# A third input unit in the prologue of a hybrid GLA and pooling block, its own weight place and banks, and another form of the input layer norm

## The reference

```python
xp = layer_norm(x_prompt, ln_in_g, ln_in_b)
xs = layer_norm(x_sample, ln_in_g, ln_in_b)
mod_ctx = jax.nn.silu(c_ctx) @ w_ada[l] + b_ada[l]       # 2048 x 12288
mod_lat = (jax.nn.silu(c) @ w_ada[l] + b_ada[l])[:, None, :]

def block(x, mod, ...):
    sh1, sc1, g1, sh2, sc2, g2 = jnp.split(mod, 6, axis=-1)
    h = x * (1 + sc1) + sh1
    m, s_f, s_b = mixer(h, ...)                          # z = h @ w_in, GLA heads, pooling, @ w_out
    x = layer_norm(ALPHA * x + g1 * m, ln1_g, ln1_b)
    h = x * (1 + sc2) + sh2
    gate, up = jnp.split(h @ w_gu, 2, axis=-1)
    f = (jax.nn.silu(gate) * up) @ w_down
    return layer_norm(ALPHA * x + g2 * f, ln2_g, ln2_b), s_f, s_b

def layer_norm(x, g, b):
    mu = jnp.mean(x, -1, keepdims=True); var = jnp.mean(jnp.square(x - mu), -1, keepdims=True)
    return (x - mu) * lax.rsqrt(var + LN_EPS) * g + b
```

## Time and profile before

| | before |
|---|---|
| median of 3 runs | 2828.46 us |
| profiled execution | 2833.38 us |
| its span | 2831.6 us |
| TensorE busy | 2714.7 us (96%) |
| VectorE busy | 1447.6 us (51%) |
| ScalarE busy | 912.9 us (32%) |
| GpSimd busy | 659.9 us (23%) |
| granted TensorE clock, mean | 0.98 |

### The profile page before, as it was taken

How to read it: one execution, slowest core, us unless ns; L and a number is a source line. 1 busy time by engine, 2 the same in 40 slices (tenths; PEclk the granted TensorE clock), 3 DMA queues, 4 the chain that set the end, 5 groups by cost and what they waited for, 6 DMA issues and landing times.

```text
span 2831.6 us, 37813 instructions
## 1 busy us (share of the span) xinstructions
PE 2714.7 (96%) x16304; PEld 2421.9 (86%) x16304; DVE 1447.6 (51%) x1582; ACT 912.9 (32%) x952; POOL 659.9 (23%) x220
## 2 busy tenths in 40 slices
PE   5798999999998999999999999999999999999997
PEld 2577788879886887999999999999999888888876
DVE  5222232224566547565555565665566545544578
ACT  5232232323222116333333333333333333223343
POOL 0000000000000000344443444444344333333440
PEclk8899999999999997999999999999999999999998
DMA  8864555542247323233333222333322845464576
GB/s 329 297 243 158 184 204 182 202 153 76 97 133 245 127 75 126 82 99 104 104 104 104 89 93 95 104 104 104 104 93 86 292 169 204 171 215 179 178 243 240
DMA packets 179385, 438.13 MB, mean 155 GB/s; under 512 B 9980, under 2 KB 25732, under 8 KB 173076
## 3 DMA queue, kind: packets, MB, share of 16 engines
q1 hardware_dynamic: 176916, 430.48, 44.2%
q10 hardware_dynamic: 2304, 5.24, 0.5%
HBM read 401.83 MB, written 33.85 MB: 154 GB/s over the span
## 4 chain that ended last, share of the span: by engine, by line
PE 56%; DMA 12%; POOL 12%; DVE 11%; issue 4%; ACT 4%; SPq 0%; POOLq 0%; ACTq 0%; DVEq 0%
DMA raw_w<-w_gu_b 7%; PE ps L2175 6%; PE ps L2176 6%; PE ps L2177 6%; PE ps L1845 5%; PE ps L1847 5%; PE ps L1846 5%; PE ps L1898 4%; PE ps L2096 4%; PE ps L2097 4%; PE ps L2098 4%; POOL raw_w L849 4%; DVE w_lo L1503 3%; POOL raw_w L852 3%; POOL low L846 3%
## 5 line engine op out<-in xcount | busy, mean ns | idle before, releaser
L1503 DVE TENSOR_TENSOR w_lo<-raw_w,w_hi 128x1024 fp32r<-128x1024 f32 x264 | 359.3, 1362 | 307.8 <-ACT w_hi L1101 305.3
L1101 ACT ACTIVATE w_hi<-raw_w 128x1024 fp32r<-128x1024 f32 x264 | 269.8, 1054 | 631.6 <-POOL raw_w L855 382.3
L2096 PE MATMUL ps<-x_hi,w_hi 128*128 128x320 f32 x1408 | 437.4, 311 | 3.5 <-DVE w_lo L1503 3.3
L2097 PE MATMUL ps<-x_lo,w_hi 128*128 128x320 f32 x1408 | 436.0, 310 | 0.0
L2098 PE MATMUL ps<-x_hi,w_lo 128*128 128x320 f32 x1408 | 436.0, 310 | 0.0
L846 POOL TENSOR_TENSOR low<-raw_w 128x1024 f32<-128x1024 f32 x42 | 104.1, 2478 | 1091.3 <-DMA raw_w<-w_gu_b 1091.3
L1634 DVE TENSOR_TENSOR x_lo<-low,x_hi 128x2560 fp32r<-128x2560 f32 (+2 forms) x55 | 221.1, 4023 | 260.9 <-ACT x_hi L1186 260.9
L1845 PE MATMUL ps<-x_hi,w_hi 128*128 128x320 f32 x1056 | 343.5, 325 | 6.8 <-DVE x_lo L1306 5.0
L2175 PE MATMUL ps<-w_hi,x_hi 128*128 128x512 f32 x880 | 343.1, 390 | 6.4 <-DVE x_lo L1634 2.4
L2176 PE MATMUL ps<-w_lo,x_hi 128*128 128x512 f32 x880 | 342.4, 389 | 0.0
L2177 PE MATMUL ps<-w_hi,x_lo 128*128 128x512 f32 x880 | 342.4, 389 | 0.0
(11 more groups left out here) (203 smaller groups left out, 4379.1 us busy)
## 6 DMA issues: line engine op xcount, KB each, us to landing
raw_w<-w_gu_b SPq DMA_DIRECT2D x180, 512.0 KB, 5.6
low<-w_ada SPq DMA_DIRECT2D x60, 1024.0 KB, 5.3
raw_w<-w_down SPq DMA_DIRECT2D x55, 1024.0 KB, 5.1
low<-hidden_scratch SPq DMA_DIRECT2D x33, 1280.0 KB, 6.1
raw_w<-w_in_b SPq DMA_DIRECT2D x33, 1024.0 KB, 7.4
high<-w_ada SPq DMA_DIRECT2D x22, 1024.0 KB, 5.4
raw_w<-w_out SPq DMA_DIRECT2D x16, 1024.0 KB, 5.1
x_raw<-w_ada SPq DMA_DIRECT2D x14, 1024.0 KB, 9.4
```

Source lines behind the costliest of these rows:

```text
L1101: nc.scalar.activation(weight(0, w), src, ACT.Copy).then_inc(prod_hi, 1)
L1503: nc.vector.tensor_tensor(weight(1, n), src, weight(0, n).bitcast(F32), ALU.subtract).then_inc(prod_split, 1)
L2096: mm(out, wh, version(v, 0, k), start=first and k == 0, stop=False)
L2097: mm(out, wh, version(v, 1, k), start=False, stop=False)
```

## The change

The third unit (unit 2) joins units 0 and 1 in the prologue (`EARLY = 3`).

- Its parts lie in a place of their own, `low_r` from column 12288 (`W_THIRD`), where the token tiles 1 and 2 were; so its split waits for all turns (`turned` 20). It accumulates in banks 4 and 5 from the start of the second block on, behind `turned_out` 20. Units from 3 on use slot (u - 1) % 2 of `w_hi` and `w_lo`, and all later stages are shifted by one slot likewise.
- Modulation sums use bank 6 alone, and `first_cols` uses bank 7, two column groups in turn. `first_cols(i)` waits for `mod_cols` i, and a new group for the copy of the one before.
- The 32 slices go through six places listed in `FIRST_SLOT`: four at first, slot 4 (one token tile) in place of slot 3 from slice 8, slot 5 (`raw_w[:, 0]`, after unit 2 is split) in place of slot 2 from slice 19, and three places (0, 5, 4) from slice 24 on.
- The order of loads: token tiles 0 and 1, then slices, with the other token tiles after slices 0, 4 and 6, and units 0 to 3 after slices 1, 3, 9 and 27; then unit 4. Tiles are turned after slices 1, 3, 5, 6 and 8.
- The quarters of units 0, 1 and 2 follow slices 3, 5 and 7 of each block from the second.
- Slots 1 and 2 of the second ring overlap unit 2's place, so their first loads wait for `unit_used` 3.
- The input norm: ScalarE takes a square root, VectorE the reciprocal and minus mean times it, ScalarE the Identity.
- ScalarE's order: roots and normalisations of the five tiles, with `first_row(0)` and the split of unit 0 after tile 1, that of unit 1 after tile 3, then `first_row(1)` and the split of unit 2. VectorE: rests of units 0 and 1 after the copies of tiles 2 and 3, that of unit 2 after those of tile 4, ahead of the first `add_bias`.

```diff
@@ -160,8 +160,12 @@
...
 ADA = [(2, "row", 0), (4, "col", SC), (3, "col", SH), (5, "row", 1)]
-X_AFTER = {0: 1, 1: 2, 3: 3, 5: 4}
-TURN_AFTER = {0: 0, 1: 1, 3: 2, 4: 3, 6: 4}
+X_AFTER = {0: 2, 4: 3, 6: 4}
+UNIT_AFTER = {1: 0, 3: 1, 9: 2, 27: 3}
+TURN_AFTER = {1: 0, 3: 1, 5: 2, 6: 3, 8: 4}
+FIRST_SLOT = (0, 1, 2, 3, 0, 1, 2, 3, 4, 0, 1, 2, 4, 0, 1, 2, 4, 0, 1, 5, 4, 0, 1, 5, 4, 0, 5, 4, 0, 5, 4, 0)
+EARLY = 3
+W_THIRD = 12288
 N_ADA = 16
@@ -328,7 +332,15 @@
...
-        return 2 * n + half if n < 2 else (2 * (n - 2) + half) % 3
+        if n < 2:
+            return 2 * n + half
+        return 4 + half if n < EARLY else (2 * (n - EARLY) + half) % 3
...
+    def w_part(part, u):
...
+        if u == 2:
+            return low_r[:, W_THIRD + UNIT * part:W_THIRD + UNIT * part + UNIT]
+        return (w_hi, w_lo)[part][:, u if u < 2 else (u - 1) % 2, :]
@@ -355,18 +367,15 @@
...
             return first_ring[:, at:at + STEP].rearrange("p (k c) -> p k c", k=4)
-        return lo(S_X + (i - 4) * STEP, STEP).rearrange("p (k c) -> p k c", k=4)
...
-    def first_slot_of(i):
...
-        return i % 4 if i < 8 else (4, 5, 6, 0)[i % 4]
+        src = lo(S_X, STEP) if i == 4 else raw_w[:, 0, :]
+        return src.rearrange("p (k c) -> p k c", k=4)
...
-    FIRST_USES = [[i for i in range(FIRST_STEPS) if first_slot_of(i) == n] for n in range(7)]
+    FIRST_USES = [[i for i in range(FIRST_STEPS) if FIRST_SLOT[i] == n] for n in range(6)]
@@ -585,12 +596,14 @@
...
-            n = first_slot_of(i)
+            n = FIRST_SLOT[i]
             before = [j for j in FIRST_USES[n] if j < i]
...
                 sp.wait_ge(first_used, before[-1] + 1)
-            elif n >= 4:
-                sp.wait_ge(turned, (16, 20, 12)[n - 4])
+            elif n == 4:
+                sp.wait_ge(turned, 16)
+            elif n == 5:
+                sp.wait_ge(split_done, 3)
             group, part = SECTIONS[i // 4 % 2][0], i // 8
@@ -605,22 +618,27 @@
...
                 sp.wait_ge(ada_used, i - RING + 1)
+            elif i:
+                sp.wait_ge(unit_used, EARLY)
             sp.dma_start(ring_slot(i), w_ada_v[ADA[a // 4][0], a % 4, i % 4]).then_inc(ada_in[i % RING], 16)
         load_x(0)
-        load_unit(0, w_in_b[0])
+        load_x(1)
         for i in range(FIRST_STEPS):
...
                 load_x(X_AFTER[i])
-            if i == 0:
-                load_unit(1, w_in_b[1])
-        load_unit(2, w_in_b[2])
+            if i in UNIT_AFTER:
+                load_unit(UNIT_AFTER[i], w_in_b[UNIT_AFTER[i]])
+        sp.wait_ge(first_used, FIRST_USES[5][-1] + 1)
+        load_unit(4, w_in_b[4])
         sp.wait_ge(h_split, KT)
...
             g = scan_index(a, b)
+            if kind == "main" and b == 2 and a < 2:
+                continue
             if kind == "main" and b == 2 and a + 3 < N_IN:
@@ -874,27 +892,28 @@
...
             act.wait_ge(raw_in[s], 16 * (u // 2 + 1))
-            if u >= 2:
-                act.wait_ge(unit_used, u - 1)
-            nc.scalar.activation(w_hi[:, s, :], raw_w[:, s, :], ACT.Copy).then_inc(w_hi_done, 1)
+            if u == 2:
+                act.wait_ge(turned, 4 * TT)
+            elif u >= 3:
+                act.wait_ge(unit_used, u - 2 if u < 5 else u - 1)
+            nc.scalar.activation(w_part(0, u), raw_w[:, s, :], ACT.Copy).then_inc(w_hi_done, 1)
...
-        def deviation(t):
-            link(nc.scalar.activation(mv(t, 2), mv(t, 1), ACT.Ln, bias=cols(C_EPS, 1)))
-            link(nc.scalar.activation(mv(t, 2), mv(t, 2), ACT.Exp, scale=-0.5))
-            link(nc.scalar.activation(mv(t, 3), mv(t, 0), ACT.Copy, scale=mv(t, 2)))
-            link(nc.scalar.activation(mv(t, 3), mv(t, 3), ACT.Copy, scale=-1.0))
...
-        def normalise(t, tile, moments_done, n):
...
-            act.wait_ge(moments_done, n)
-            deviation(t)
-            nc.scalar.activation(tile, tile, ACT.Identity, bias=mv(t, 3),
-                                 scale=mv(t, 2)).then_inc(normed, 1)
+        def in_rooted(t):
...
+            act.wait_ge(moments, t + 1)
+            nc.scalar.activation(mv(TT + t, 2), mv(TT + t, 1), ACT.Sqrt, bias=cols(C_EPS, 1)).then_inc(in_root, 1)
...
+        def in_normalise(t):
...
+            act.wait_ge(in_scale, t + 1)
+            tile = lo(S_X + (t % 3) * D, D)
+            nc.scalar.activation(tile, tile, ACT.Identity, bias=mv(TT + t, 3),
+                                 scale=mv(TT + t, 2)).then_inc(normed, 1)
@@ -902,17 +921,21 @@
...
                 act.wait_ge(mod_turned, i - 1)
-            nc.scalar.activation(high[:, at:at + 512], ps[:, 6 + i % 2, :], ACT.Copy).then_inc(mod_rows, 1)
...
-        normalise(TT, lo(S_X, D), moments, 1)
-        split_in(0)
-        normalise(TT + 1, lo(S_X + D, D), moments, 2)
-        split_in(1)
-        for t in range(2, TT):
-            normalise(TT + t, lo(S_X + (t % 3) * D, D), moments, t + 1)
+            nc.scalar.activation(high[:, at:at + 512], ps[:, 6, :], ACT.Copy).then_inc(mod_rows, 1)
...
+        for t in range(TT):
+            in_rooted(t)
+            in_normalise(t)
+            if t == 1:
+                first_row(0)
+            if t in (1, 3):
+                split_in(t // 2)
+        first_row(1)
+        split_in(2)
         for q in range(4):
-            first_row(2 * q)
-            first_row(2 * q + 1)
+            if q:
+                first_row(2 * q)
+                first_row(2 * q + 1)
             for k in range(4 * q, 4 * q + 4):
@@ -998,7 +1021,8 @@
...
                 evac(a)
-                split_in(a + 2)
+                if a != 2:
+                    split_in(a + 3 if a < 2 else a + 2)
             elif kind == "vT":
@@ -1277,6 +1300,10 @@
...
             nc.vector.bn_aggr(mv(TT + t, 0, 2), cols(C_STAT + 24 * (t % 2), 24)).then_inc(moments, 1)
+            dve.wait_ge(in_root, t + 1)
+            link(nc.vector.reciprocal(mv(TT + t, 2), mv(TT + t, 2)))
+            nc.vector.scalar_tensor_tensor(mv(TT + t, 3), mv(TT + t, 0), -1.0, mv(TT + t, 2), ALU.mult,
+                                           ALU.mult).then_inc(in_scale, 1)
@@ -1307,21 +1334,20 @@
...
         ln_in(0)
-        split_rest(0)
-        ln_in(1)
-        evac_turned(0)
-        split_rest(1)
-        for t in range(2, TT):
+        for t in range(1, TT):
             ln_in(t)
             evac_turned(t - 1)
+            if t >= 3:
+                split_rest(t - 3)
         evac_turned(TT - 1)
+        split_rest(2)
         for q in range(4):
...
                 add_bias(section, q, mod_col[:, section, 4 * q:4 * q + 4, :],
-                         ps[:, 4 + g, 0:8].rearrange("p (k c) -> p k c", c=2), mod_cols)
+                         ps[:, 7, 8 * g:8 * g + 8].rearrange("p (k c) -> p k c", c=2), mod_cols)
             dve.wait_ge(mod_cols, 2 * q + 2)
@@ -1832,16 +1858,16 @@
...
                     first, last = b == 0 and k % 4 == 0, b == 3 and k % 4 == 3
-                    wh = w_hi[:, n % 2, k * P:(k + 1) * P]
-                    wl = w_lo[:, n % 2, k * P:(k + 1) * P]
+                    wh = w_part(0, n)[:, k * P:(k + 1) * P]
+                    wl = w_part(1, n)[:, k * P:(k + 1) * P]
                     out = ps[:, main_bank(n, half), 0:HALF]
...
                     xl = x_lo[:, k, half * HALF:(half + 1) * HALF]
-                    if n < 2 and half == 0:
+                    if n < EARLY and half == 0:
                         pe.wait_ge(h_split, k + 1)
-                    if n >= 2 and first:
-                        i = 2 * (n - 2) + half
-                        pe.wait_ge(zin_evac, 1 if i < 2 else 2 if i == 2 else 3 + (i - 3) // 2)
+                    if n >= EARLY and first:
+                        i = 2 * (n - EARLY) + half
+                        pe.wait_ge(zin_evac, 1 if i < 2 else 2 if i == 2 else 4 + (i - 3) // 2)
                     mm(out, wh, xh, start=first, stop=False)
@@ -1854,45 +1880,37 @@
...
             pe.wait_ge(sums_ready, 1)
-            if i < 2:
-                pe.wait_ge(turned_out, 4 * TT)
-            else:
-                pe.wait_ge(mod_cols, i - 1)
+            if i:
+                pe.wait_ge(mod_cols, i)
             for k in range(4):
                 c = PRO_ROW + 512 * (i % 2) + k * P
-                ins = mm(ps[:, 4 + i % 2, 2 * k:2 * k + 2], high[:, c:c + P], group_sum,
+                at = 8 * (i % 2) + 2 * k
+                ins = mm(ps[:, 7, at:at + 2], high[:, c:c + P], group_sum,
                          start=True, stop=True)
...
-        used = [0] * 7
+        used = [0] * 6
         for i in range(FIRST_STEPS):
-            n = first_slot_of(i)
+            n = FIRST_SLOT[i]
             used[n] += 1
-            q, g, m = i // 8, i // 4 % 2, i % 4
+            q, m = i // 8, i % 4
             pe.wait_ge(first_in[n], 16 * used[n])
-            if m == 0 and q:
-                pe.wait_ge(mod_rows, 2 * (q - 1) + g + 1)
-            ada_step(6 + g, first_slot(n), m, first_used)
+            if m == 0 and i:
```

(50 more changed lines are left out.)

## The result

The changed kernel takes 2843.13 us, the median of six runs (2839.70 to 2845.13), against 2828.16 us before (six runs); the ratio is 1.0051 with a 95% interval of 1.0040 to 1.0062. So it is 15 us slower. The direction was as forecast; the size was not: 2835.8 was said, with 2842 as the upper end.

What follows compares the result with a forecast made beforehand. TensorE, 96% busy, was taken to bound the kernel by its matmul order. The prologue to the end of `first_cols(7)` cost +10.4 us, the tail -3.1: +7.3, so 2835.8 us on the median 2828.46; range 2824 to 2842.

Steps and rivals of the forecast that it cites:

- The knot: Before the first block: `first_cols(1)` waits for VectorE's first bias, queued behind the split of unit 2; ends at 66.4 us.
- e1: End of `first_cols(1)` in the prologue, forecast at 66.4 us (65.8 to 67.5).
- e7: End of `first_cols(7)`, forecast at 138.0 us against 127.6 before: +10.4 us.
- The pace of a block: Prologue blocks between `first_cols` ends: TensorE's order, with h tiles awaited, takes 23.5 us, over the 21.7 of loads.
- rival C: Clock falls in every prologue block, 5.1 us instead of 1.5: +10.9, 2839.4 us; chance 0.16.
- Rival A: Loads go on setting the prologue's pace, TensorE's waits overlapping them better: -2.6, 2825.9 us; chance 0.18.
- The tail: From the end of `first_cols(7)` to unit 3's first matmul: 32.7 us against 35.8, so -3.1 us, ring wait included.
- T3: End of unit 2's last quarter, where ring loads may be issued; forecast 19.3 us after `first_cols(7)` ends.
- priced at nothing: Side effects taken as 0, among them one more exp table load before the first gate (0 to 1.3 us).
- the last step of the sum: Whole kernel: +7.3 us laid on the traced execution makes 2840.7 us, on the median 2828.46 makes 2835.8.
- main(3,0): First quarter of unit 3, after the ring's four steps; forecast to start near 170 us, everything later following one to one.
- B: Loads set the pace and TensorE keeps 2.4 GHz through the last quarters: -6.8, 2821.7 us; chance 0.14.

Runs made afterwards that it cites:

- the kernel with the knot cut: Changed kernel with the split of unit 2 (ScalarE and VectorE) moved behind the first four h tiles: 2839.25 us, ratio 1.0039.
- the second trace: The changed kernel run once more, unaltered, for a second trace and more times: median 2842.62 us, ratio 1.0056.
- the quarters left out: Changed kernel without computing the first three quarters of unit 2: 2836.41 us, ratio 1.0034.
- free ring kernel: Changed kernel with first loads of second-ring steps 1 to 3 put in places unit 2 does not use: 2831.62 us, ratio 1.0015.
- three edits: Changed kernel with second ring from quarter 12, unit 2's split behind four h tiles, rests of units 0 and 1 behind tile 3's copies: 2816.50 us, ratio 0.9965.

## Why the forecast had the sign and missed the size

**The knot held, but came later than said.** e1 was to be 66.4 (65.8 to 67.5) and was 68.97; in four other traces of the same prologue it was 67.6 to 68.3. The mechanism is that of the forecast, row by row, and the kernel with the knot cut confirms it. The term mis-sized is the queue before it: turned 16 came at 52.1, not 49.9, since tile 2 was turned from 39.83 on, after a slice at half clock (1.88 us), and VectorE's copies ended at 43.9 instead of 42.1; F8 landed at 57.18 instead of 55.0. That is 2.2 of the 2.6 us, and 2.4 of them reached e7 (140.45 instead of 138.0). The forecast's own addition before e1, 60.6 + 1.9 + 2.3 + 0.2, makes 65.0 and not 65.2; nothing hangs on it.

**The pace of a block held.** Said were 23.5 us and e7 - e1 = 71.6 with 1.5 for the clock. Measured: 24.15, 24.15 and 23.2 us, together 71.5. The clock was at full from 72.7 to 144.4 us, so rival C is refuted for this execution. The half clock of the first 3.7 us of the first block cost nothing that shows, as the second block, at full clock, took as long. So that the total came out right is luck in part: the 1.5 us put down for the clock were spent on two blocks 0.6 us longer each than worked out. In the second trace C happened in part. Rival A (loads set the pace) is refuted by the 309 GB/s and by the quarters left out, which would have gained nothing.

**The tail held.** T3 - e7 was 18.1 instead of 19.3, unit 3 started 12.7 after T3 instead of 12.4, and the half clock behind it took 1.6 instead of 1.0: together 32.4, where 32.7 were forecast. T3 came sooner because the clock was at half for 6.8 us in the last quarters and not for 10.2; in the second trace it was 10.2 again, and T3 - e7 19.1. The free ring kernel shows the wait directly: 11 us, as much as the 11 us of quarters that were moved out of this stretch. Free ring (11 us) and cut knot (3.9) are together the 15 us by which the kernel is slower, if they add; what is left of the change then neither wins nor loses anything that the medians show.

**One thing priced at nothing was not.** The exp table that the old norm left loaded must now be loaded before the first gate: that wait of TensorE for ScalarE was 0.88 us and is 1.7 (waits from 170 us on), and the shift grows there by 0.8 us, from 9.4 to 10.1. The new norm alone in the kernel before shows the same wait of 1.7 us.

```profile
PE ps L2034 <- ACT low L1033: 1.7, 1, 1.7
```

**What failed is the last step of the sum, and two terms before it.** The medians lie 15.0 us apart, where 7.3 were said: 7.7 are missing.

The last step made a difference between traces, +7.3, and laid it on the median by taking the same 4.9 us off both kernels. But an execution's distance from its median is not the same in both. The first trace of before stands 5.2 us above the median of its six runs, that of the changed kernel 2.0 above its own (it is the longest of its six), and the second ones 7.7 and 0.6. That is 3.2 of the missing 7.7 us. In the forecast's own terms, 2840.7 was said for a traced execution and 2845.13 and 2843.19 were measured, 4.4 and 2.5 more.

The 4.4 us of the first trace are terms of the sum. The queue before the knot, in the norm stage, was 2.4 us too short. The tail was 0.4 too long. And "everything later follows main(3,0) one to one, to within 1 us" was 2.4 us too low: 0.8 for the table, and 1.8 that came in small steps between 600 us and the end, less 0.2 between. These 1.8 us are not shown to be of the change: in the second trace the shift shrinks there, from 13.2 to 10.2 us.

So one trace was no base to 0.2%, and the range should have had some 5 us more on its upper side. What sets the length of an execution from 600 us on stays open.

**The rival of the other side** (B, faster by 6.8) needed e7 by 130 us; the earliest with all three units computed was 134.4, after three edits.

## What to carry to other kernels

Moving work under loads pays only if nothing that was issued beside it is now issued behind it: here 11 us of quarters were moved, and the ring that shared their storage made TensorE wait 11 us at a place where it had nothing else to do. When a shorter chain (the norm) or a split is put into an engine's queue, look at what stands behind it there, in order; two such places were mended by moving a few lines, for 6 to 7.6 us together. And before laying a difference from one trace on a median, look where that trace stands among the runs.

## What the runs showed of the hardware

The granted clock made the largest difference between the two traced executions of the changed kernel in the prologue: in the same blocks it stayed at 1.00 for 71.7 us in one and fell to 0.51 twice for 3.4 us in the other, both times while a quarter's matmuls came one h tile at a time. Where loads depend on TensorE's use of their places, such a stretch can cost more than what it slows: in the kernel before a slice that took 0.8 us longer at half clock was followed, twelve microseconds on, by a wait for a load that was 1.6 us longer than in an execution without it.

A lone load of 1 MB landed 5.0 us after its issue (5.1 in the earlier trace rows); those in the queue behind it followed 2.7 us apart (TensorE's waits for the three slices of the ring end at 163.92, 166.64 and 169.34 us).

The same 2.2 ms of program, from 600 us to the end, took 2221.1 to 2234.9 us in eight executions, a spread of 13.8 us or 0.5% of the whole.
